# Gated values turned in 32x32 squares by VectorE in place of whole turns on TensorE, in a one-core decoder layer

## The reference

```python
merged = (jax.nn.sigmoid(gate_a) * (y_attn @ w_branch_attn[l])
          + jax.nn.sigmoid(gate_b) * (y_rwkv @ w_branch_rwkv[l]))
x = x + merged @ w_out[l]
h = rms_norm(x, norm_ffn[l])
x = x + (jax.nn.silu(h @ ffn_gate[l]) * (h @ ffn_up[l])) @ ffn_down[l]
...
return rms_norm(x, norm_final)
```

## Time and profile before

| | us |
|---|---|
| median of 3 runs | 2778.48 (2775.72 to 2781.59) |
| the profiled execution | 2777.86 |
| its span, first to last instruction | 2776.0 |
| TensorE busy | 2730.2 (98%), mean granted clock 0.997 |
| VectorE busy | 1798.3 (65%) |
| ScalarE busy | 1267.3 (46%) |
| GpSimd busy | 639.2 (23%) |

### The profile page before, as it was taken

One profiled execution on the slowest core, in us unless ns is written; L12 is line 12 of the kernel. 1 busy time (PEld: TensorE's weight loads), 2 busy tenths in 40 slices (PEclk: granted clock), 3 DMA queues, 4 the chain that ended last, 5 costly groups with the idle time before them and its releaser, 6 DMA issues.

```text
span 2776.0 us, 37866 instructions
## 1 busy us (share of the span) xinstructions
PE 2730.2 (98%) x14290; PEld 2204.4 (79%) x14290; DVE 1798.3 (65%) x2947; ACT 1267.3 (46%) x2110; POOL 639.2 (23%) x487
## 2 busy tenths in 40 slices
PE   8999999999999999999999999999999999999997
PEld 7777777777777777888887888888888888888876
DVE  5656365364463554432258878887788789888886
ACT  5444343343333334222345555555555556556555
POOL 2323234243333343554440000000000000111112
PEclk9999999999999999999999999999999999999999
DMA  5222122222222223443445665446545677787784
GB/s 189 76 76 105 64 84 94 76 88 79 76 84 83 78 97 110 160 155 129 136 132 160 178 178 153 143 160 178 145 130 162 178 215 213 190 255 179 197 215 109
DMA packets 190611, 382.51 MB, mean 138 GB/s; under 512 B 9584, under 2 KB 84592, under 8 KB 175728
## 3 DMA queue, kind: packets, MB, share of 16 engines
q1 hardware_dynamic: 145808, 319.76, 33.3%
q0 software_dynamic: 29728, 45.09, 9.9%
q10 hardware_dynamic: 14912, 15.47, 1.6%
HBM read 328.91 MB, written 51.38 MB: 137 GB/s over the span
## 4 chain that ended last, share of the span: by engine, by line
PE 91%; DVE 3%; ACT 2%; issue 1%; DMA 1%; DVEq 1%; POOL 0%; ACTq 0%; SPq 0%; POOLq 0%
PE dense L2037 12%; PE work L2430 11%; PE work L2432 11%; PE work L2434 11%; PE dense L2039 11%; PE dense L2038 11%; PE dense L2430 3%; PE dense L2432 3%; PE dense L2434 3%; PE work L2205 1%; PE work L2443 1%; PE work L2257 1%; ACT whi L821 1%; DVEq L1313 1%; PE work L2037 1%
## 5 line engine op out<-in xcount | busy, mean ns | idle before, releaser
L821 ACT ACTIVATE ring_hi<-wblock 128x512 fp32r<-128x512 f32 x840 | 529.7, 632 | 526.0 <-PE work L2434 350.2
L759 POOL TENSOR_TENSOR wlo<-raw,whi 128x512 fp32r<-128x512 f32 x400 | 541.1, 1383 | 896.4 <-ACT whi L821 896.4
L1756 DVE TENSOR_TENSOR ring_lo<-wblock,ring_hi 128x512 fp32r<-128x512 f32 x840 | 575.9, 689 | 166.5 <-ACT ring_hi L821 157.7
L2430 PE MATMUL work<-ring_hi,S_hi 128*128 128x512 f32 x1460 | 572.0, 392 | 6.9 <-DVE ring_lo L1756 6.8
L2432 PE MATMUL work<-ring_hi,S_lo 128*128 128x512 f32 x1460 | 568.9, 390 | 0.0
L2434 PE MATMUL work<-ring_lo,S_hi 128*128 128x512 f32 x1460 | 568.8, 390 | 0.0
L2037 PE MATMUL dense<-H_hi,whi 128*128 128x512 f32 x1208 | 504.8, 418 | 10.0 <-DVE H_lo L1341 8.5
L2039 PE MATMUL dense<-H_hi,wlo 128*128 128x512 f32 x1208 | 473.2, 392 | 0.0
L2038 PE MATMUL dense<-H_lo,whi 128*128 128x512 f32 x1208 | 473.0, 392 | 0.0
L821 ACT ACTIVATE whi<-raw 128x2048 fp32r<-128x2048 f32 (+1 forms) x109 | 198.2, 1821 | 473.7 <-PE dense L2039 388.3
L2430 PEld LDWEIGHTS work<-ring_hi,S_hi 128*128 128x128 f32 x1460 | 274.4, 188 | 69.5 <-DVE ring_lo L1756 7.3
(11 more groups left out here) (337 smaller groups left out, 3409.4 us busy)
## 6 DMA issues: line engine op xcount, KB each, us to landing
raw<-w_slots SPq DMA_DIRECT2D x101, 1024.0 KB, 4.9
wblock<-w_gu SPq DMA_DIRECT2D x88, 1024.0 KB, 9.7
wblock<-w_down SPq DMA_DIRECT2D x60, 512.0 KB, 7.1
wblock<-w_gu POOLq DMA_DIRECT2D x22, 1024.0 KB, 9.9
S_raw<-s_dram SPq DMA_DIRECT2D x14, 1024.0 KB, 7.5
tight<-w_down SPq DMA_DIRECT2D x20, 512.0 KB, 8.6
gates_dram<-gout ACTq DMA_DIRECT2D x32, 256.0 KB, 2.1
gin<-gates_dram SPq DMA_DIRECT2D x16, 512.0 KB, 3.7
```

What stands on the lines that cost most here:

```text
L759: done = nc.gpsimd.tensor_tensor(wlo[s][:, at], raw[s][:, at], whi[s][:, at].bitcast(f32), SUB)
L821: return A.activation(dst, src, ACT.Copy, scale=scale)
L1756: V.tensor_tensor(ring_lo[w % RING][:], of_tile(j, source[product], k), ring_hi[w % RING][:].bitcast(f32), SUB).then_inc(ring_lo_ready, 1)
L2430: PE.matmul(banks[a][:], S_hi[product][:, k, tok], high[:], start=(k == 0 and product not in (3, 2)), stop=False, skip_group_check=True)
```

## The change

The hidden values are no longer turned on TensorE. `turn_hidden` is now VectorE's: a transpose of `[128, 512]` that turns each square of 32 by 32 in its place, so that within a square columns and tokens are swapped while the squares stay where they are. For that the buffers of a gate/up chunk are filled in another order of columns (`rows_of`, `like_rows`: four pieces of 128 columns per token half, the same number of elements). The two turns on TensorE, their waits and ScalarE's four copies go.

The sums for down are then made in that layout, and the stores put the squares in place: each operand of a chunk is stored by four DMAs, one per group of 32 partitions, in runs of 32 elements, 128 B. `s_dram` has 32 rows per operand in place of 128, and each load of `S_raw` is four DMAs with runs of 512 B. The order of the work at the seam is now: VectorE turns `c22buf` into `u3buf` in steps 1 and 2 of product 5 and `u2buf` into `c22buf` in steps 3 and 4, then makes three sums in steps 5 to 7 and the fourth in the second step of product 6, behind a wait for `s12_stored` of the same chunk.

```diff
-    s_dram = nc.dram_tensor("s_dram", (len(PRODUCTS), P, FFN_HIDDEN // 2 // P * HALF_T), f32,
+    s_dram = nc.dram_tensor("s_dram", (len(PRODUCTS), P // 4, 4 * FFN_HIDDEN // 2 // P * HALF_T), f32,
...
+        def rows_of(j, buf, a):
+
+            if j >= CHUNKS:
+                return buf[:, a, :]
+            return buf[:].rearrange("p x (c s n) -> p (x c) s n", s=2, n=P)[:, :, a, :]
...
-            def store_s(j, product, buf, stored):
-
-                cols = slice(j * CHUNK_F, (j + 1) * CHUNK_F)
-                rows = s_dram[S_ROWS[product]:S_ROWS[product] + 2][:, :, cols]
-                sp.dma_start(rows.rearrange("a p c -> p a c"), buf[:]).then_inc(stored, 16)
+            def store_s(j, product, piece, stored):
+
+                cols = s_dram[S_ROWS[product]][:, 4 * j * CHUNK_F:4 * (j + 1) * CHUNK_F]
+                placed = cols.rearrange("i (x q n) -> q i x n", q=4, n=32)
+                for q in range(4):
+                    sp.dma_start(placed[q], piece[32 * q:32 * (q + 1), :].rearrange("i (x n) -> i x n", n=32)
+                                 ).then_inc(stored, 16)
...
-                sp.dma_start(S_raw[product][:, 0:count, :], cols.rearrange("p (k t) -> p k t", t=HALF_T)
-                             ).then_inc(s_loaded[product], 16)
+                found = cols.rearrange("i (x b n) -> b i x n", b=4, n=P)
+                for b in range(4):
+                    into = S_raw[product][32 * b:32 * (b + 1), 0:count, :]
+                    sp.dma_start(into.rearrange("i k (s n) -> i (k s) n", n=P), found[b]
+                                 ).then_inc(s_loaded[product], 16)
...
-                if 0 < j <= CHUNKS:
-                    sp.wait_ge(c_read, copied(j - 1, "out1"))
-                    store_s(j - 1, 1, u2buf, s12_stored)
...
                 if 0 < j <= CHUNKS:
+                    sp.wait_ge(c_ready, part(j - 1, "t2"))
+                    store_s(j - 1, 4, u3buf[:, 1, :], s64_stored)
+                    sp.wait_ge(c_ready, part(j - 1, "t1"))
+                    store_s(j - 1, 2, c22buf[:, 1, :], s12_stored)
+                    store_s(j - 1, 1, c22buf[:, 0, :], s12_stored)
                     sp.wait_ge(c_ready, part(j - 1, "sa"))
-                    store_s(j - 1, 5, c22buf, s57_stored)
-                    sp.wait_ge(c_ready, part(j - 1, "sb", 0))
-                    store_s(j - 1, 6, u3buf, s64_stored)
-                    sp.wait_ge(c_ready, part(j - 1, "sb", 1))
-                    sp.dma_start(s_dram[S_ROWS[3]][:, (j - 1) * CHUNK_F:j * CHUNK_F], u2buf[:, 1, :]
-                                 ).then_inc(s3_stored, 16)
+                    store_s(j - 1, 5, u2buf[:, 0, :], s57_stored)
+                    store_s(j - 1, 7, u2buf[:, 1, :], s57_stored)
+                    sp.wait_ge(c_ready, part(j - 1, "sb"))
+                    store_s(j - 1, 6, u3buf[:, 0, :], s64_stored)
+                    store_s(j - 1, 3, c22buf[:, 1, :], s3_stored)
...
                             if seam:
-                                act.wait_ge(s12_stored, 16 * j)
-                                act.wait_ge(s3_stored, 16 * j)
+                                act.wait_ge(s57_stored, S_PAIR * j)
...
+            def turn_hidden(into, hidden, half):
+
+                fence()
+                V.transpose(into[:, half, :], hidden[:, half, :]).then_inc(c_ready, 1)
...
+                if i == 3:
+                    dve.wait_ge(s12_stored, S_PAIR * (j + 1))
+                    fence()
+                    V.tensor_tensor(c22buf[:, 1, :], c22buf[:, 1, :], u3buf[:, 0, :], SUB).then_inc(c_ready, 1)
...
-                    if seam and k in (3, 4, 5, 6):
-                        s_of_hidden(j - 1, k)
+                    if seam and k in (0, 1):
+                        turn_hidden(u3buf, c22buf, k)
+                    if seam and k in (2, 3):
+                        turn_hidden(c22buf, u2buf, k - 2)
+                    if seam and k in (4, 5, 6):
+                        s_of_hidden(j - 1, k - 4)
...
+                    if seam and k == 1:
+                        s_of_hidden(j - 1, 3)
...
-                gate_up_items(j, 7, range(4))
                 if seam:
-                    pe.wait_ge(c_ready, part(j - 1, "hid2"))
-                    turn_hidden(bank_b, c22buf).then_inc(hid_turned, 1)
-                gate_up_items(j, 7, range(4, n))
+                    pe.wait_ge(c_ready, part(j - 1, "hid1"))
...
-                if not down:
-                    pe.wait_ge(c_ready, part(j, "hid1"))
-                    turn_hidden(bank_d, u2buf).then_inc(hid_turned, 1)
```

More of the change, by code:

```diff
@@ L91 @@
 assert sum(GROUP_PAIRS) * 2 * P == FFN_HIDDEN
+S_PAIR = 16 * 2 * 4
 S_ROWS = {1: 0, 2: 1, 5: 2, 7: 3, 6: 4, 4: 5, 3: 6}
@@ L683, in load_s @@
                 sp.wait_ge(item_done, after(j, product))
-                cols = s_dram[S_ROWS[product]][:, 8 * g * HALF_T:(8 * g + count) * HALF_T]
-                sp.dma_start(S_raw[product][:, 0:count, :], cols.rearrange("p (k t) -> p k t", t=HALF_T)
-                             ).then_inc(s_loaded[product], 16)
+                cols = s_dram[S_ROWS[product]][:, 32 * g * HALF_T:4 * (8 * g + count) * HALF_T]
+                found = cols.rearrange("i (x b n) -> b i x n", b=4, n=P)
[3 more added lines that the diff above has]
+                                 ).then_inc(s_loaded[product], 16)
             sp.wait_ge(tile_done, DOWN0 - 1)
@@ L1137, in silu_gate2 @@
                 act.wait_ge(c_ready, part(j, "c21", a))
[L1138 removed]
+                A.activation(rows_of(j, u3buf, a), rows_of(j, u3buf, a), ACT.Silu,
                              scale=rstd[:, 2 + a:3 + a]).then_inc(c_read, 1)
[L1141 to L1149 removed]
             def sums_of_a(j, a):
@@ L1206, in _ @@
                     for e in events(j, k):
-                        if seam and e in (3, 4):
-                            turned1_out(j - 1, e - 3)
                         if seam and e in (6, 7):
@@ L1223, in _ @@
                     ring_high(j, 5, k)
-                    if seam and k in (1, 2):
-                        turned2_out(j - 1, k - 1)
                     if j == 0 and k == 4:
@@ L1239, in _ @@
                             if seam:
-                                act.wait_ge(s12_stored, 16 * j)
-                                act.wait_ge(s3_stored, 16 * j)
+                                act.wait_ge(s57_stored, S_PAIR * j)
                             elif j:
                                 act.wait_ge(added[12], 16 * (j - CHUNKS))
-                            copy(u2buf[:, e - 4, :], bank_of(j, 1)[e - 4][:]).then_inc(c_read, 1)
+                            copy(rows_of(j, u2buf, e - 4), like_rows(j, bank_of(j, 1)[e - 4])
+                                 ).then_inc(c_read, 1)
                     if last and k == 0:
@@ L1827, in s_of_hidden @@
+            def turn_hidden(into, hidden, half):
+                fence()
+                V.transpose(into[:, half, :], hidden[:, half, :]).then_inc(c_ready, 1)
+            def s_of_hidden(j, i):
+                if i == 0:
                     fence()
-                    V.tensor_tensor(u3buf[:, 0, :], c22buf[:, 0, :], u2buf[:, 0, :], SUB).then_inc(c_ready, 1)
-                if e == 6:
-                    dve.wait_ge(s12_stored, 16 * (j + 1))
+                    V.tensor_tensor(u2buf[:, 0, :], u3buf[:, 0, :], u3buf[:, 1, :], ADD).then_inc(c_ready, 1)
+                if i == 1:
+                    V.tensor_tensor(u2buf[:, 1, :], c22buf[:, 0, :], u3buf[:, 0, :], SUB).then_inc(c_ready, 1)
+                if i == 2:
@@ L1934, in _ @@
                             if seam:
[L1935 removed]
+                                dve.wait_ge(s64_stored, S_PAIR * j)
                             elif j:
@@ L2444, in turn_halves @@
                 return done
-            def turn_hidden(banks, buf):
-                return turn_halves(banks, [buf[:, a, :] for a in range(2)])
             def s_wait(j, product):
@@ L2456, in _ @@
             for j in range(LAST):
-                n, seam, down = depth(j), 0 < j <= CHUNKS, j >= CHUNKS
+                n, seam = depth(j), 0 < j <= CHUNKS
                 if j:
@@ L2471, in _ @@
                     pe.wait_ge(c_read, copied(j - 1, "c11"))
+                if seam:
+                    pe.wait_ge(c_ready, part(j - 1, "hid1"))
                 s_wait(j, 7)
-                gate_up_items(j, 7, range(4))
-                if seam:
-                    pe.wait_ge(c_ready, part(j - 1, "hid2"))
-                    turn_hidden(bank_b, c22buf).then_inc(hid_turned, 1)
-                gate_up_items(j, 7, range(4, n))
+                gate_up_items(j, 7, range(n))
                 if j == 0:
```

78 lines of the change are left out of this document (30 added, 48 removed).

## The result

The changed kernel takes 2809.3 us (median of 4 runs, 2807.1 to 2812.1) against 2778.5 for the kernel before: a ratio of 1.0113, 95% interval 1.0099 to 1.0127. That is 30.8 us slower where I had forecast 2.6. It lies in the range of 2765 to 2850, and 28.8 us from the forecast of 2780.5. The profiled execution has a span of 2805.3 us against 2776.0.

A forecast was written before the change was run, and what follows sets the result against it. The prediction took TensorE to bound the chunk loop, with VectorE just behind in one place. Turns −12.3, first down step +2.0, stores +9.9 and S loads +3.0 gave +2.6 on 2777.86: 2780.5 us, range 2765 to 2850.

The forecast's parts named there:

- The turns, −12.3: Gate/up chunks: dropping TensorE's two turns per chunk gains 1.12 us each over 11 chunks, 12.3 us, below the 19.4 ceiling.
- The last rival: VectorE's lag at product 7's fourth step doesn't bind: all 19.4 us gained, 2773 or 2763 us; chance 0.03.
- The transposes cost nothing: Product 5, first four steps: VectorE's four transposes per chunk fit in its lead of 1.9 us, costed at nothing.
- the rival of 1.2 us: A VectorE transpose takes 1.2 us, using up the lead: 0.6 to 1.5 us per chunk, 2787 to 2797; chance 0.06.
- +2.0: First down step: VectorE has no lead, four operations of 0.77 us added, 1.1 in idle time, 2.0 us lost once.
- The stores, +9.9: Product 6: VectorE's and ScalarE's waits for small-run stores stall 0.9 us per chunk, 9.9 us over 11 chunks.
- 1645.9 + 5.6 + 396 × 0.0142: Landing of 12 store DMAs: first packet, accumulating load's remaining work, 396 packets at 14.2 ns; 1657.1, semaphore 0.5 later.
- the stalls of 0.7 and 0.2: Product 6, per chunk: 0.7 us from VectorE's wait for 12 DMAs, 0.2 from ScalarE's wait for 20.
- S loads, +3.0: Down steps: S loaded by four DMAs in 512 B rows costs 1 us per pass over three passes, ends 0 and 8.
- In time: Stores land in time, packet at 10.6 to 12 ns meeting both waits: 2770.6 us, 2767 to 2773; chance 0.28.
- A packet of nearly the price of 512 B: A 128 B store packet costs nearly a 512 B one: 2808 us at 18 ns, 2851 at 24 ns; chance 0.24.
- Doubled small writes: 128 B store runs written by reading and writing back, 48 ns instead of 24: 23 us per chunk, near 3025; chance 0.06.

The follow-up runs named there:

- e2: Changed kernel with one store per product in 2 KB rows and one load per product and group, placement of squares left out at both: 2768.3 us.
- e13: e11 with VectorE's two hidden2 moved to the seventh and eighth step of product 7 in chunks 1 to 9: 2763.6 us.
- e3: Changed kernel with GpSimd's accumulating load left out in chunks 1 to 10, stores as they are: 2777.9 us.
- e5: Changed kernel with GpSimd's accumulating load issued in four parts of 0.5 MB from the second step of product 7 on: 2794.1 us.
- e1: Changed kernel with its 28 stores per chunk in rows of 2 KB instead of 128 B runs, placement of squares left out: 2782.7 us.
- e10: e4 with SP's loads of earlier sums (fin) behind the last block 11's load and S_hi of product 7 one step later: 2775.4 us.
- e11: e10 with GpSimd's accumulating load in four parts of 0.5 MB, as in e5; nothing left out: 2768.0 us.
- e4: Changed kernel with VectorE's last sum moved to product 6's seventh step and ScalarE's two copies of product 1 to its seventh and eighth: 2782.4 us.

## Why the prediction was right and wrong, point by point

**The turns, −12.3: right.** 1.12 us per chunk expected, 1.16 measured (e2). The lag at the fourth step of product 7 is there as worked out. In the changed kernel the timeline of TensorE reads, to be held against the earlier trace rows:

```profile
1716.23 0.39 PE L2447 MATMUL work<-ring_lo,S_hi 128*128 128x512 f32 x1
1716.59 0.50 PE L2443 MATMUL work<-ring_hi,S_hi 128*128 128x512 f32 x1
...
1717.85 0.40 PE L2447 MATMUL work<-ring_lo,S_hi 128*128 128x512 f32 x1
1718.46 0.51 PE L2443 MATMUL work<-ring_hi,S_hi 128*128 128x512 f32 x1 [0.21 <-DVE ring_lo L1754]
```

0.13 + 0.38 us of waiting and 0.11 for each restart make 0.73, where the kernel before lost 0.28 and I forecast about 0.9 (0.28 and the 0.63 that turn into a wait). The last rival, that the lag doesn't bind, is out: e13 had to move hidden2 to get that part.

**The transposes cost nothing: right.** 0.71 us each; a step with one takes 1.38 us on VectorE (1723.50 to 1724.88) where I said 1.39. The estimate worked out from the Trainium skill, "VectorE: DVE Perf Modes", The three transpose paths, was 0.71 us, and the trace agrees; the rival of 1.2 us is out. At the first down step I had +2.0; the gaps of TensorE at 2374 to 2380 (0.30, 0.73, 0.53 and 0.72, with three restarts) are 1.7.

**The stores, +9.9: wrong, and this is the step that failed.** It lies in the line "1645.9 + 5.6 + 396 × 0.0142", in which the load's remaining work is added to that of the packets and packets set the pace behind it, and in the stalls of 0.7 and 0.2 that come out of it. Measured from the second transpose's end (1725.6), the 12 DMAs landed after 13.1 us and the 20 after 18.0 (1738.71 and 1743.61), where I had 12.6 and 16.4. For 20 DMAs the parts are:

- the hold by the accumulating load: 20 issues took 16.0 us in place of 20 × 0.53 = 10.6, so 5.4 us, where I had 5.6. That term was about right, though not as a sum of work: for the first 3.6 us the stores had no packet on the engines (0.9 without the load), and then the queues took turns by the packet.
- the pace: 10.6 us for 20 issues of SP, where I had 9.4 of packets. With the true price of 11.6 ns packets would need 7.7. The packet was cheaper than I said (11.6 in place of 14.2), and it didn't matter, since SP issued one DMA per 0.53 us and left a third of the engines idle. I had SP's 0.46 us in hand from the earlier trace rows and never multiplied it by 20. It would have given 9.2, no more than the packets, so that alone would not have saved the forecast: a DMA of 512 runs takes 0.53, which no row of before shows.
- from the last issue to the landing: 2.0 us, where I had 0.9 + 0.5.

e3 (load away, stall away) and e5 (load earlier, 15 us less) show the hold; the engines' 67% and 74%, and e1's 0.43 us per issue with a sixteenth of the packets, show the pace. But e1 also shows that the hold hangs on the run: on the mean of chunks 1 to 9 the 20 DMAs have landed 17.8 us behind the first issue in the changed kernel, 16.7 in e5, 13.7 in e3 and 13.8 in e1. Taking away the load alone, or the short runs alone, brings the landing 4 us forward. My sum priced the hold by the load's own work, whatever the runs beside it.

The stall itself: VectorE's 1.2 us on the mean of the first eight full chunks where I had 0.7, ScalarE's 1.0 where I had 0.2. I had counted neither the two restarts of 0.11 nor the clock. 1.6 us more on the 20 DMAs is nearly all stall, since the slack was used up. With the restarts and the clock, and the stalls of chunk 10, where loads of S come on top, it is 1.89 + 1.16 = 3.05 us per chunk in place of 0.9. That is 30.5 us over the ten chunks of the ledger in place of 9.

**S loads, +3.0: too small, and past its end of 8.** From the last chunk's product 7 on 10.1 us are lost, 1.7 of it at the first down step. Each of the three stalls hangs on SP's queue. I counted the loads' own delay and gave nothing for what stands behind them: a block that ScalarE wants first of all, and for which it waited 4.0 us before, now takes 8 us behind four loads of S and fin (2.3 to 3.3 in e10, e11 and e13, with fin behind the block).

**The rivals.** *In time*: out as built, though its packet price (10.6 to 12 ns) was the true one. *A packet of nearly the price of 512 B*: it gave 2808 at 18 ns, which is the time that came, by another mechanism; the packet's price excludes it. *Doubled small writes*: out. By the Trainium skill, "DMA: Bandwidth & Descriptors", Specifications, a transfer below 512 B is a read-modify-write; the trace has 11.6 ns for stored packets of 128 B beside 24 for 512 B, so no doubling is seen, and the measurement decides. 

## What to carry to other kernels

Many small DMAs are priced by their issuer first: what is left of a large load ahead of them, then the number of issues times the time of one, then the last one's landing; the packets' price decides only where it is more than that. Beside a large load short runs cost more than their bytes, since in these traces the queues took turns by the packet. Where a change adds a wait, look at how far that wait can be moved before looking at what it waits for: here a sum and two copies moved by a few steps gave back 26 of 31 us. And of transfers on one queue, put the one that is wanted first ahead, above all when the change makes those in front of it longer.

## What the runs showed that I had not expected

**The clock.** Behind the long stalls TensorE runs at half clock. By stretch, behind the stall of 2.56 us at 2062.42, behind that of 5.68 at 2681.93, and between the two stalls of 1.30 and 1.44 shown above:

```profile
2065.90:2068.80 2.90, 2.90 (x8) 2.24 (x7) 1.93 (x4) 0.98 (x2) 0.00 (x0) 0.50 0.79 154
...
2687.70:2691.50 3.80, 3.80 (x9) 3.02 (x10) 3.80 (x7) 3.80 (x9) 0.00 (x0) 0.50 0.80 263
1740.00:1744.00 4.00, 3.94 (x17) 3.27 (x18) 1.21 (x3) 0.40 (x1) 0.00 (x0) 1.00 0.73 125
```

0.50 is 1.2 GHz, 1.00 is 2.4. Matmuls then follow each other at 0.43 us; the eight behind the first stall cost 8 × 0.2 = 1.6 us, the fourteen or so behind the second 2.8. With the 1.5 behind a stall of 3.07 at 2300.23 that is some 6 us of the 30 that no term of my sum held, and it makes the stall of 2.56 us cost 4. Not every such stall has it: behind one of 2.73 us in e4 (2272.89) and one of 2.56 in e5 (1818.70) the clock stayed at 1.00. Between 1490 and 2700 us the changed kernel has 13.6 us at half clock, e1 10.2, e4 6.8 and e11 none.

**The stores' pace.** Some 900 to 1050 packets of 128 B per us, 0.12 to 0.13 MB, from one issuing engine, with the DMA engines otherwise idle; and 64 KB in rows of 2 KB is issued only 0.08 us sooner than 64 KB in runs of 128 B.
